# A two-layer fp32 block on one core: the queues of DVE, ACT and PE at three layer boundaries put in another order

## The reference

```python
mod = c_act @ w_ada + b_ada                       # six vectors: shift, scale, gate, twice
h = modulate(rmsnorm(x, g_norm_mix), sh1, sc1)    # rows over their root mean square, then affine
y = mixer(h @ w_in) @ w_out                       # block 1: recurrence and pooling; block 2: two attentions
x = x + gt1 * y
h = modulate(rmsnorm(x, g_norm_ffn), sh2, sc2)
f = (silu(h @ w_gate) * (h @ w_up)) @ w_down      # 2048 -> 5632 -> 2048
x = x + gt2 * f                                   # block 1 ends with one more rmsnorm
```

## Time and profile before

| | |
|---|---|
| runs, median (lowest to highest) | 2757.09 us (2756.20 to 2758.58) |
| the profiled execution, its own time | 2759.05 us |
| its span | 2757.4 us |
| PE busy | 2505.6 us, 91% |
| DVE busy | 1867.1 us, 68% |
| ACT busy | 1135.9 us, 41% |
| mean granted clock of PE | 0.965 |

### The profile page before, as it was taken

One profiled execution on the slowest core, in us unless ns is written; L12 is line 12 of the kernel. 1 busy time (PEld: TensorE's weight loads), 2 busy tenths in 40 slices (PEclk: granted clock), 3 DMA queues, 4 the chain that ended last, 5 costly groups with the idle time before them and its releaser, 6 DMA issues.

```text
span 2757.4 us, 34513 instructions
## 1 busy us (share of the span) xinstructions
PE 2505.6 (91%) x13446; PEld 2158.2 (78%) x13446; DVE 1867.1 (68%) x1808; ACT 1135.9 (41%) x1303; POOL 258.0 (9%) x418
## 2 busy tenths in 40 slices
PE   1199788999999999998999999888999999999999
PEld 1198666788888888886999999787778888888887
DVE  6778797677777778766776445765557755555556
ACT  2044433433333333344344556344443343444333
POOL 2313521011111111000110000000001000000000
PEclk9599898999999999998999999999999999999999
DMA  9887596688888888754895555234548755555554
GB/s 335 308 300 267 206 341 238 203 298 316 301 300 300 301 303 303 269 184 137 317 335 188 168 164 158 77 122 152 200 165 300 255 193 189 193 183 191 187 170 153
DMA packets 290575, 639.03 MB, mean 232 GB/s; under 512 B 21755, under 2 KB 34557, under 8 KB 290077
## 3 DMA queue, kind: packets, MB, share of 16 engines
q1 hardware_dynamic: 236112, 440.61, 47.1%
q0 software_dynamic: 53792, 196.63, 19.6%
q10 hardware_dynamic: 556, 0.18, 0.0%
HBM read 635.28 MB, written 2.10 MB: 231 GB/s over the span
## 4 chain that ended last, share of the span: by engine, by line
PE 74%; DVE 11%; DMA 4%; ACT 4%; issue 4%; POOL 2%; ACTq 0%; DVEq 0%; POOLq 0%
PE PS L1566 73%; DMA R<-in_w_ada 4%; DVE WLO L942 3%; DVE R L962 3%; ACT WHI L516 2%; ACT R L603 1%; DVE R L1460 1%; PE PS L1729 1%; POOL YF L461 1%; DVE HID L1164 0%; POOL YF L460 0%; POOL YF L465 0%; DVE H L1103 0%; DVE H L987 0%; POOL R L467 0%
## 5 line engine op out<-in xcount | busy, mean ns | idle before, releaser
L942 DVE TENSOR_TENSOR WLO<-RAW,WHI 128x1024 fp32r<-128x1024 f32 x816 | 1002.2, 1232 | 693.1 <-ACT WHI L516 691.6
L516 ACT ACTIVATE WHI<-RAW 128x1024 fp32r<-128x1024 f32 x816 | 857.9, 1060 | 1138.7 <-PE PS L1566 1133.5
L1566 PE MATMUL PS<-WHI,H 128*128 128x512 f32 x3488 | 1104.9, 398 | 66.8 <-DVE WLO L942 50.3
L1566 PEld LDWEIGHTS PS<-WHI,H 128*128 128x128 f32 x3488 | 657.5, 191 | 228.5 <-DVE WLO L942 61.2
L1566 PE MATMUL PS<-WLO,H 128*128 128x512 f32 x1744 | 687.8, 394 | 0.0
L1566 PE MATMUL PS<-H,WHI 128*128 128x256 f32 x3168 | 593.9, 289 | 40.6 <-DVE WLO L942 34.7
L1566 PEld LDWEIGHTS PS<-H,WHI 128*128 128x128 f32 x3168 | 504.5, 196 | 51.2 <-DVE WLO L942 42.2
L962 DVE SCALAR_TENSOR_TENSOR R<-R,CA 128x1024 f32<-128x1024 f32 x360 | 465.1, 1292 | 43.5 <-DMA R<-in_w_ada 37.3
L1566 PE MATMUL PS<-H,WLO 128*128 128x256 f32 x1584 | 453.9, 287 | 0.0
L1566 PE MATMUL PS<-WHI,HID 128*128 128x512 f32 x1280 | 396.2, 391 | 1.4 <-DVE WLO L942 1.4
L1566 PEld LDWEIGHTS PS<-WLO,H 128*128 128x128 f32 x1744 | 332.9, 191 | 71.5
(11 more groups left out here) (194 smaller groups left out, 1032.0 us busy)
## 6 DMA issues: line engine op xcount, KB each, us to landing
R<-in_w_ada POOLq DMA_DIRECT2D x368, 512.0 KB, 6.5
RAW<-in_w_in SPq DMA_DIRECT2D x88, 1024.0 KB, 5.6
RAW<-in_w_ffn_in SPq DMA_DIRECT2D x88, 1024.0 KB, 5.0
RAW<-in_w_ffn_gate SPq DMA_DIRECT2D x44, 1024.0 KB, 7.4
RAW<-in_w_ffn_up SPq DMA_DIRECT2D x44, 1024.0 KB, 5.2
RAW<-in_w_ffn_down SPq DMA_DIRECT2D x44, 1024.0 KB, 10.5
RAW<-in_w_ffn_out SPq DMA_DIRECT2D x44, 1024.0 KB, 5.2
RAW<-in_w_out SPq DMA_DIRECT2D x32, 1024.0 KB, 5.8
```

What stands on the lines that cost most here:

```text
L516: nc.scalar.activation(WHI[j][:, :, :], RAW[slot][:, 2 * half:2 * half + 2, :], ACT.Copy)\
L942: nc.vector.tensor_tensor(WLO[j][:, :, :], RAW[slot][:, 2 * half:2 * half + 2, :], WHI[j][:, :, :].bitcast(F32), ALU.subtract).then_inc(lo ...
L1566: return nc.tensor.matmul(o, a, b, start=start, stop=stop, skip_group_check=True)
```

## The change

The operations stay the same. Four things change place: DVE's `lo` among the pieces (`lo N` behind `last_half 0`, `x_hat` 4 ahead of `to_h` 2, `lo N+3`, `x_hat` 6 and 7 ahead of `to_h` 4, and `lo N+4`, `lo N+5` together ahead of `to_h` 6); ACT's `hi N+3` ahead of `to_ft` 4, and `hi N+5` inside the boundary; PE's `turn 2` into the middle of pass one, between its half on sub N and its half on sub N+1; and in the last 16 subs of a feed-forward part the gate, sum and gain of chunks 1 and 2. The loops behind the boundaries start at sub 6 in place of 5, since one more sub is split inside.

```diff
--- before.py
+++ after.py
@@ -621,6 +621,7 @@
                 to_ft(2)
                 hi()
                 to_ft(3)
+                hi()
                 to_ft(4)
                 to_ft(5)
                 hi(2)
@@ -687,8 +688,9 @@
                         squares((s - 9) // 2, x_step, 4 + (s - 9) // 2 + 1)
                     if s in (10, 12) and final:
                         squares_gained((s - 10) // 2)
+                    if s == 14 and final:
+                        squares(2, x_step, 4 + 3)
                     if s == 15 and final:
-                        squares(2, x_step, 4 + 3)
                         squares_gained(2)
 
 
@@ -796,9 +798,9 @@
 
             w_out_squares(0, 0)
             boundary(1, 10, mod_at(0, 3), "DC")
-            ffn(1, 5, final=True)
+            ffn(1, 6, final=True)
             boundary(2, 16, mod_at(1, 0), "DB")
-            for s in range(5, 16):
+            for s in range(6, 16):
                 hi()
                 if s == 9:
                     copy_out("A", tiles(24, 4))
@@ -920,7 +922,7 @@
             split([(free["A"], A_LAT + 2), (free["B"], B_LAT + 2)], first=0)
             w_out_squares(2, 8)
             boundary(3, 22, mod_at(1, 3), "DC")
-            ffn(3, 5)
+            ffn(3, 6)
             assert c.unit.at == N_UNITS
 
 
@@ -1107,8 +1109,8 @@
 
                 end = c.sub.value()
                 to_h = lambda n: h_piece(k, n)
+                last_half(pair, k - 1, 0, freed, end)
                 lo()
-                last_half(pair, k - 1, 0, freed, end)
                 stats(k, 0, squares)
                 inverse(k, 0)
                 x_hat(0)
@@ -1121,17 +1123,17 @@
                 lo()
                 to_h(1)
                 x_hat(3)
+                x_hat(4)
                 to_h(2)
-                x_hat(4)
                 lo()
+                x_hat(5)
                 to_h(3)
-                x_hat(5)
-                to_h(4)
-                to_h(5)
                 lo()
                 x_hat(6)
                 x_hat(7)
-                lo()
+                to_h(4)
+                to_h(5)
+                lo(2)
                 to_h(6)
                 to_h(7)
 
@@ -1249,12 +1251,12 @@
                         product()
                     if s == 4:
                         hidden(HID_LAST)
-                    if s in (7, 10, 13):
-                        last_gated((s - 7) // 3)
-                    if s in (8, 11, 14):
-                        last_added((s - 8) // 3)
-                    if s in (9, 12, 15) and k == 1:
-                        last_gained((s - 9) // 3)
+                    if s in (7, 9, 13):
+                        last_gated((7, 9, 13).index(s))
+                    if s in (8, 10, 13):
+                        last_added((8, 10, 13).index(s))
+                    if s in (9, 11, 14) and k == 1:
+                        last_gained((9, 11, 14).index(s))
 
 
             nc.vector.memset(PRAW[:, BLOCKS - 1, :], 0.0).then_inc(praw_zero, 1)
@@ -1343,11 +1345,11 @@
                             ada_end()
             modulation(COL["g_norm_ffn"], mod_at(0, 4), 10)
             boundary("B", 1, 5, 8)
-            ffn(mod_at(0, 5), 1, A_FFN1, C_FFN1, 12, 5, (0, 1))
+            ffn(mod_at(0, 5), 1, A_FFN1, C_FFN1, 12, 6, (0, 1))
 
             modulation(COL["g_norm1_2"], mod_at(1, 1), 16, COL["g_norm_final"])
             boundary("C", 2, C_FFN1, 16)
-            for s in range(5, 16):
+            for s in range(6, 16):
                 lo()
                 if 7 <= s < 15:
                     tb, q = divmod(s - 7, 4)
@@ -1551,7 +1553,7 @@
                         residual("BA"[g % 2], 2, g - 1, (A_PROJ if g % 2 else B_PROJ) + 1 + g // 3)
             modulation(COL["g_norm2_2"], mod_at(1, 4), 22)
             boundary("B", 3, B_PROJ + 2, 21)
-            ffn(mod_at(1, 5), 3, A_END, C_END, 24, 5, (1, None))
+            ffn(mod_at(1, 5), 3, A_END, C_END, 24, 6, (1, None))
             end = c.sub.value()
             for tb in range(2):
                 last_half("C", 3, tb, C_END, end)
@@ -1595,7 +1597,8 @@
                 c.sub.at += 1
                 used.at += last and counted
 
-            def by_tokens(pair, src, k0, first, before=lambda tb: None, counted=True):
+            def by_tokens(pair, src, k0, first, before=lambda tb: None, middle=lambda: None,
+                          counted=True):
 
 
                 used, o, js = c.all[pair], PAIR[pair], [ring(c.sub.at + i)[0] for i in range(2)]
@@ -1605,6 +1608,8 @@
                     before(tb)
                     for i in range(2):
                         if tb == 0:
+                            if i == 1:
+                                middle()
                             pe.wait_ge(lo_done, c.sub.value(i + 1))
                         for k in range(2):
                             kk = k0 + 2 * i + k
@@ -1633,11 +1638,13 @@
                         if tb == 0:
                             pe.wait_ge(ada_bias, c.ada_group.value())
                             pe.wait_ge(gt_row, 4 * k)
-                        for n in (2 * tb, 2 * tb + 1):
-                            turn(k, n, pairs)
+                            turn(k, 0, pairs)
+                            turn(k, 1, pairs)
+                        else:
+                            turn(k, 3, pairs)
                         pe.wait_ge(h_tb, base + 2 * tb + 1)
 
-                    by_tokens(pair, src, 0, True, before)
+                    by_tokens(pair, src, 0, True, before, lambda: turn(k, 2, pairs))
                     turn(k, 4, pairs)
                     turn(k, 5, pairs)
                     begin = 2
```

## The result

The change makes the kernel 1.3% faster, as predicted.

What follows compares the result with a forecast made beforehand. PE bounds the kernel, losing time to queue order at layer boundaries. Gains 32.6 + 0.8 - 0.1 + 5.1 = 38.4 us take the profiled 2759.05 to 2720.7; the median, 1.96 lower, is forecast at 2719 us, range 2712 to 2730.

Steps and rivals of the forecast that it cites:

- What bounds the kernel: PE, busy 91% of the span; three gaps alike in every layer boundary, ended by order of queues, not quantity of work.
- Inside the boundary: First product to sub N+6 takes 21.7 us in each boundary, winning 12.0, 10.2 and 10.4 us, together 32.6 us.
- half clock of pass one: First products of the new stage: 5.12 us in the sum, the last triple at full clock, some 0.3 us off.
- The gap before pass two: PE's 2.35 us wait for DVE's split of a piece becomes about 0.5 us.
- The sentence on 0.6: Sign in the timeline after: no PE idle over 0.6 us between the first product and N+6.
- N+3, N+5, N+6: Subs inside the boundary: both 2.12 us gaps on `lo` go; 2.4 us to spare at N+3, 0.3 at N+6, the tightest.
- Fronts: Stretches ahead of each boundary's first product: 0.8 us won at the first, 5.1 at the second, 0.1 lost at the third.
- Things costed at nothing: Earlier DMAs: zero, up to 2 us lost; last 16 subs of the second feed-forward part: zero, up to 1.1 lost.
- The clock: Rival: remaining 0.5 us gap and front cause one more half-clock stretch per boundary, 4.8 us, giving 2724; chance 0.13.
- The waits change their name: Rival: ACT becomes the last, gaps before N+3 and N+5 stay; 22 us taken back, giving 2741; chance 0.08.
- It doesn't do what it says: Rival: the ring of three lets no `hi` go ahead, only the fronts gain; 2751; chance 0.02.
- Slower, by PE in order: Rival: late x_hat 2 holds PE behind `turn` 2 in each boundary, past 1.4 us to spare; 2763; chance 0.02.

Runs made afterwards that it cites:

- p_alone: The kernel before, with only `turn` 2 moved into the middle of pass one; median 2746.93 us.
- o_alone: The kernel before, with only the order of pieces and splits on DVE and of `hi N+3` on ACT changed; median 2735.57 us.
- one_more_on_dve: The kernel after, plus one DVE addition that nobody reads, behind the split of piece 7; median 2725.48 us.
- f_alone: The kernel before, with only the last 16 subs of the feed-forward part changed (gate, sum, gain, squares earlier); median 2752.10 us.
- l_alone: The kernel before, with only `lo N` moved behind `last_half 0`; median 2754.18 us.
- all_but_o: The kernel after, with the order of pieces, splits and `hi N+3` on DVE and ACT put back; median 2744.15 us.
- after_again: The kernel after, unchanged, run once more beside three others on the same chip; median 2723.62 us.
- front_filled: The kernel after, with products of old data in PE's idle stretches ahead of each boundary's first product; median 2719.65 us.
- turn2_first: The kernel after, with `turn` 2 ahead of the whole of pass one; median 2723.32 us.

## Why the prediction was right

**What bounds the kernel.** Right. The three gaps of each boundary were matters of order, and all three were shut by order alone. p_alone removed the first (all but 0.95 us of it) and left the other two, o_alone did the reverse: two causes, each with its own cure, as forecast.

**Inside the boundary.** 31.78 us against 32.6, and the kind was right too: 18.29 us of idle time (three times "some 6 us") and 13.49 us of work at half clock (14.6 forecast). The sum took 5.12 us for a pass one at half clock, where its own rows give 5.20; that is too little to matter. The term that was off is the *half clock of pass one*. The clock was taken to come back towards its end, for 21.7 us in each. In the second boundary it came back in the middle of pass one, for 21.65; in the third all of pass one ran at half clock and only pass two ran at full clock (granted clock 0.64 in 1965 to 1970), for 22.13.

**The gap before pass two.** It was forecast at 0.5, with no idle over 0.6 us. Measured 0.59, 0.97 and 0. The sentence on 0.6 failed in the second boundary, for a reason that costs nothing: pass one went faster there, and PE came earlier to the split that it waits for. Pass two began 6.57, 6.09 and 6.56 us behind the first product, so the boundary with the longest wait was the quickest.

**N+3, N+5, N+6.** No waits, as walked. In the third boundary `lo N+3` had 2.39 us to spare (2.4 forecast) and `lo N+5` 2.98; N+6 had 0.46 us in the first and 0.50 in the third (0.3), and one_more_on_dve showed that this place is indeed the next to turn into a wait.

**Fronts.** 0.82 for 0.8, 5.04 for 5.1, -0.31 for -0.1. At the second, `last_half` came 4.84 us earlier (4.4 to 4.9 forecast), and both parts of the reasoning were tested: f_alone took away PE's 1.36 us and brought `last_half` 4.53 us forward, and l_alone brought it 2.80 forward without touching them. The first alone gives nearly all of the front, which the forecast didn't need to know, since it costed them together. The expectation for all_but_o failed by 3 to 6 us for another reason: its fronts came as forecast (4.94 us at the second), but inside the boundaries it took 2.65 us more than p_alone, with the third at a granted clock of 0.78 against 0.94.

**Things costed at nothing.** Earlier DMAs cost nothing that shows. 0.69 us was given back between the second and the third boundary. From N+6 of the second to the first product of the third it is 700.84 us in the kernel before, 701.84 in the kernel after and 700.97 in its repeat, after_again. So most of it varies with the execution; its cause was not sought.

**The rivals.** *The clock*: the granted clock rose in all three boundaries, so the 4.8 us weren't lost. But its other half was true: the idle fronts still cost clock, and front_filled won some 3 us from just that. *The waits change their name*: ACT's wait for `turn` fell by 26.2 us, and no wait of PE rose by more than 0.4 us. *It doesn't do what it says*: refuted by the timeline. *Slower, by PE in order*: the mechanism exists, as turn2_first shows, though most of its wait was won back there, and it needs a scaled piece that comes late. In the kernel after it came at 1963.54, 1.54 us ahead of `turn` 2 at 1965.08 (1.4 forecast).

## What to carry to other kernels

When several engines wait in turn for each other at the seam of two stages and none is busy, take each gap of the bounding engine, follow what released it back to the instruction that stood in a queue behind something it didn't need, and move that one; here about 37 us came from a few such moves with no instruction less. Cost such a gap with the work behind it, since here the clock came back late (all of pass one of the third boundary ran at half of it): about a third of what was won was clock. And where idle time in PE can't be closed, products of old data in it can buy back the clock (13.4 us in the kernel before, some 3 us in the kernel after), as long as they don't hold up what comes next: the 18 ahead of the first boundary gave back all that they won.

## What was not expected of the hardware

- A gap of 2.12 us in a busy PE was enough to leave half clock behind it in one place (the gap before 2008.57), and the same gap ten microseconds later was not. Windows of PE behind the gap that ends at 2018.85 in the kernel before, and behind the one that ends at 2002.26 in all_but_o, where half clock does follow:

```profile
2019.00:2020.00 1.00, 1.00 (x5) 1.00 0.17 29
2020.00:2021.00 1.00, 1.00 (x6) 1.00 0.78 160
```

```profile
2003.00:2004.00 1.00, 1.00 (x4) 0.60 0.75 72
2004.00:2005.00 1.00, 1.00 (x3) 0.50 0.87 324
```

The same order of instructions at the same boundary gave 31.33 us in one execution and 33.74 in another, and the same order behind the first product 26.72 and 30.15. So a price for the clock behind one given gap is good only as a mean over several.
- The program ahead of the first boundary, unchanged, differed by up to 2.9 us between the profiled executions, as much as the smaller effects here. Distances inside the trace told parts apart that the runs' times could not.
- The gains of four independent-looking edits overlapped by some 8 of 45.5 us; 2.9 us of it are seen directly in the traces, at the front of the second boundary.
